# Scaling twelve of sixteen one-hot rows on ScalarE, one u tile ahead on TensorE, four more u tiles in the routing stage

## The reference, cut to what matters

```python
top_s, top_i = lax.top_k(s, PEER_TOPK)                 # s: (token, head, half, 128 keys)
cand_i = top_i[..., 0, :, None] * PEER_NKEYS + top_i[..., 1, None, :]
best_s, pos = lax.top_k(cand_s, PEER_TOPK)             # 16 of 256 sums
eidx = jnp.take_along_axis(cand_i, pos, axis=-1)       # expert = i * 128 + j
gate = jax.nn.softmax(best_s, axis=-1)
a = jax.nn.gelu(jnp.einsum('nd,ned->ne', xt, ue), approximate=False)   # ue = u[eidx]
out = jnp.einsum('ne,ned->nd', a * gt, ve)                             # ve = v[eidx]
```

## Time and profile before

| what | value |
|---|---|
| median of 3 runs | 1917.18 us (1903.87 to 1917.84) |
| the profiled execution | 1917.83 us; its span, first to last instruction, 1916.0 us |
| mean granted clock of PE | 0.959 of full |
| PE busy | 1762.7 us, 92% of the span |
| DVE busy | 1109.7 us, 58% |
| ACT busy | 780.1 us, 41% |
| POOL busy | 954.5 us, 50% |
| gates stage | 745.1 to about 1029 us of the span |
| experts stage | about 1030 to 1916 us |

### The profile page before, as it was taken

The page is one execution under the profiler, slowest core; times in us unless marked ns, Lnnn a source line. Parts: engine busy times, 40 slices in busy tenths (PEclk is TensorE's granted clock), DMA queues, the critical chain, the costliest instruction groups (busy, mean ns, idle before and its releaser), DMA issues. The chain is left out here.

```text
span 1916.0 us, 32083 instructions
## 1 busy us (share of the span) xinstructions
PE 1762.7 (92%) x11464; PEld 1456.3 (76%) x11464; DVE 1109.7 (58%) x2245; ACT 780.1 (41%) x1268; POOL 954.5 (50%) x743
## 2 busy tenths in 40 slices
PE   7979857979999996888998999999999999999996
PEld 5867724449998896888997877778787777878774
DVE  3662678236679999885444545554555545455453
ACT  5333326333333343434443444444444444444442
POOL 3473621006577792000003767666676666766662
PEclk9989969889999997889998999999999999999998
DMA  5211150015444463466777999999999999999995
GB/s 179 99 53 58 18 183 25 1 58 176 158 157 157 124 190 108 160 242 218 228 229 255 328 342 327 335 343 330 329 330 341 338 327 334 326 344 330 333 320 181
DMA packets 166004, 427.22 MB, mean 223 GB/s; under 512 B 23456, under 2 KB 74400, under 8 KB 165280
## 3 DMA queue, kind: packets, MB, share of 16 engines
q1 hardware_dynamic: 118992, 273.20, 43.2%
q0 software_dynamic: 45056, 134.38, 19.0%
q10 hardware_dynamic: 1872, 18.56, 2.4%
HBM read 390.02 MB, written 36.04 MB: 222 GB/s over the span
## 5 line engine op out<-in xcount | busy, mean ns | idle before, releaser
L1740 POOL DMA_INDIRECT rows<-in_peer_v,row_i x256 | 281.8, 1101 | 198.3 <-PE psum L1936 129.9
L1731 POOL DMA_INDIRECT spot<-acts_first,spot_i x256 | 300.5, 1174 | 83.0 <-issue 77.4
L1909 PE MATMUL psum<-h2hi,u_hi 128*128 128x256 f32 x1024 | 294.2, 287 | 8.6 <-DVE u_lo L1802 8.6
L1909 PE MATMUL psum<-h2lo,u_hi 128*128 128x256 f32 x1024 | 291.1, 284 | 0.0
L1909 PE MATMUL psum<-h2hi,u_lo 128*128 128x256 f32 x1024 | 290.4, 284 | 0.0
L1909 PEld LDWEIGHTS psum<-h2hi,u_hi 128*128 128x128 f32 x1024 | 195.9, 191 | 63.0 <-DVE u_lo L1802 31.5
L1919 PE MATMUL psum<-v_hi,w_lo 128*128 128x512 f32 x512 | 202.7, 396 | 0.0
L1919 PE MATMUL psum<-v_lo,w_hi 128*128 128x512 f32 x512 | 202.1, 395 | 0.0
L1919 PE MATMUL psum<-v_hi,w_hi 128*128 128x512 f32 x512 | 201.9, 394 | 0.0
L1802 DVE TENSOR_TENSOR u_lo<-u_raw,u_hi 128x1024 fp32r<-128x1024 f32 x128 | 157.5, 1231 | 71.3 <-ACT u_hi L1755 71.3
L1813 DVE TENSOR_TENSOR wgt<-gel,g_in 128x256 f32<-128x256 f32 x128 | 55.4, 433 | 246.8 <-ACT gel L1765 246.8
(11 more groups left out here) (242 smaller groups left out, 4069.3 us busy)
## 6 DMA issues: line engine op xcount, KB each, us to landing
u_raw<-in_peer_u SPq DMA_DIRECT2D x256, 512.0 KB, 4.2
v_raw<-in_peer_v SPq DMA_DIRECT2D x128, 512.0 KB, 6.6
acts_first<-gel SPq DMA_DIRECT2D x128, 128.0 KB, 2.0
gates<-chunk ACTq DMA_DIRECT2D x4, 4096.0 KB, 12.3
g_in<-gates SPq DMA_DIRECT2D x64, 256.0 KB, 2.9
wring<-in_w_in SPq DMA_DIRECT2D x24, 512.0 KB, 3.6
wq_raw<-in_w_query SPq DMA_DIRECT2D x16, 512.0 KB, 5.7
w_out<-in_w_out SPq DMA_DIRECT2D x1, 4096.0 KB, 18.7
```

The costliest lines, as they stand in the source:

```text
L1731: pool.indirect_dma_start(spot[:, t:t + 1], None, spots, bass.IndirectOffsetOnAxis(ap=spot_i[:, t:t + 1], axis=0)).then_inc(s_spot, 16)
L1740: pool.indirect_dma_start(rows[:, slot, :], None, values, bass.IndirectOffsetOnAxis(ap=row_i[:, t:t + 1], axis=0)).then_inc(s_rows[slot], 16)
L1909: last = pe.matmul(psum[:, ACTS + s % 2, 0:DENSE], a[:, s % 2, k, :], b[:, k, GATHERED:T], start=(k == 0 and a is u_hi and b is h2hi), sto ...
```

## The change

1. In a batch DVE compares twelve tokens of `hot_i` in one operation, without the gate, and ahead of `hot_j`. The other four tokens keep the instruction that compares and multiplies.
2. ACT multiplies those twelve tokens by their gates, in place, one instruction per token, with the gate as a scale on each partition (`scale`). PE waits for this too (`s_scaled`).
3. On ACT the high part of the u tile three ahead comes first in a batch, then `scale`, then Gelu, then the four copies.
4. PE does the u tile of the batch to come ahead of this batch's products; one tile is done ahead of the first batch.
5. `EARLY_ROUTING` goes from 64 to 68: four more u tiles in routing, and four fewer behind the batches (60 in the stage: 16 beside, one more ahead, 43 behind).
6. In the experts stage the four gathers of a quad share a semaphore, and PE waits once for them in place of four times.

```diff
--- before.py
+++ after.py
@@ -53,7 +53,8 @@
 BANKS = 8
 BANK = 512
 
-EARLY_ROUTING = 64
+EARLY_ROUTING = 68
+SCALED = 12
 EARLY = NKEYS
 USLOTS = 4
 QEVERY = 3
@@ -1413,7 +1414,7 @@
         hot_j = sb("hot_j", [P, 2, BATCH, P])
         hot_i = sb("hot_i", [P, 2, BATCH, P])
         chunk = sb("chunk", [P, 2, P, CHUNK])
-        s_gated, s_hot_j = sem("gated_r"), sem("hot_j_r")
+        s_hot_i, s_scaled, s_gated, s_hot_j = sem("hot_i_r"), sem("scaled_r"), sem("gated_r"), sem("hot_j_r")
         s_prod, s_moved = sem("gate_prod"), sem("gate_moved")
         s_st = keep["gates_out"]
         s_u = [sem(f"u4_in{i}") for i in range(USLOTS)]
@@ -1478,10 +1479,11 @@
             def one_hots(eng_it, b):
                 batch = eng_it * BATCHES + b
                 wait(dve, s_prod, (batch - 1) * QUADS)
-                tokens = bass.ds(batch * BATCH + GATHERED, BATCH)
-                dve.tensor_tensor(hot_j[:, b % 2, :, :], iota[:].unsqueeze(1).to_broadcast([P, BATCH, P]),
-                                  chosen[:, 1, tokens].unsqueeze(2).to_broadcast([P, BATCH, P]), ALU.is_equal).then_inc(s_hot_j, 1)
-                for s in range(BATCH):
+                for hot, row, some, ready in ((hot_i, 0, SCALED, s_hot_i), (hot_j, 1, BATCH, s_hot_j)):
+                    dve.tensor_tensor(hot[:, b % 2, 0:some, :], iota[:].unsqueeze(1).to_broadcast([P, some, P]),
+                                      chosen[:, row, bass.ds(batch * BATCH + GATHERED, some)].unsqueeze(2).to_broadcast([P, some, P]),
+                                      ALU.is_equal).then_inc(ready, 1)
+                for s in range(SCALED, BATCH):
                     one = bass.ds(batch * BATCH + GATHERED + s, 1)
                     last = dve.tensor_scalar(hot_i[:, b % 2, s, :], iota[:], chosen[:, 0, one], chosen[:, 2, one],
                                              ALU.is_equal, ALU.mult)
@@ -1517,9 +1519,10 @@
             def body(it):
                 for b in range(BATCHES):
                     batch = it * BATCHES + b
-                    activations(batch, b % USLOTS)
+                    activations(batch + 1, (b + 1) % USLOTS)
+                    pe.wait_ge(s_hot_j, batch + 1)
+                    pe.wait_ge(s_scaled, batch + 1)
                     pe.wait_ge(s_gated, batch + 1)
-                    pe.wait_ge(s_hot_j, batch + 1)
                     for q in range(QUADS):
                         wait(pe, s_moved, (batch - 1) * QUADS + q + 1)
                         for s in range(4):
@@ -1527,10 +1530,13 @@
                                              hot_i[:, b % 2, q * 4 + s, :], start=True, stop=True)
                         last.then_inc(s_prod, 1)
 
+            activations(0, 0)
             body(0)
             with pe.Fori(1, ITERS) as it:
                 body(it)
-            with pe.Fori(BESIDE, TURNS) as it:
+            for e in range(1, USLOTS):
+                activations(BESIDE * USLOTS + e, e)
+            with pe.Fori(BESIDE + 1, TURNS) as it:
                 for e in range(USLOTS):
                     activations(it * USLOTS + e, e)
 
@@ -1552,11 +1558,20 @@
                 wait(act, s_ast[e % 2], (turn * (USLOTS // 2) + e // 2) * 16)
                 act.activation(gel[:, e % 2, 0:GATHERED], psum[:, 6 + e % 2, 0:GATHERED], ACT.Gelu).then_inc(s_gel, 1)
 
+            def scale(it, b):
+                batch = it * BATCHES + b
+                act.wait_ge(s_hot_i, batch + 1)
+                for s in range(SCALED):
+                    one = bass.ds(batch * BATCH + GATHERED + s, 1)
+                    last = act.activation(hot_i[:, b % 2, s, :], hot_i[:, b % 2, s, :], ACT.Identity, scale=chosen[:, 2, one])
+                last.then_inc(s_scaled, 1)
+
             def body(it):
                 for b in range(BATCHES):
                     batch, half = it * BATCHES + b, b // HALF
+                    split_ahead(it * 2 + b // USLOTS, b % USLOTS)
+                    scale(it, b)
                     gelu(it * 2 + b // USLOTS, b % USLOTS)
-                    split_ahead(it * 2 + b // USLOTS, b % USLOTS)
                     if b % HALF == 0:
                         wait(act, s_st[half], it * 16)
                     for q in range(QUADS):
@@ -1634,7 +1649,7 @@
         s_u = [sem(f"u5_in{i}") for i in range(E)]
         s_v = [sem(f"v_in{i}") for i in range(E)]
         s_g = [sem(f"g_in{i}") for i in range(2)]
-        s_rows = [sem(f"rows_in{i}") for i in range(VG)]
+        s_rows = [sem(f"rows_in{z}") for z in range(PER)]
         s_uhi, s_ulo, s_act, s_gel = sem("u5_hi_r"), sem("u5_lo_r"), sem("act5_pe"), sem("gel5_r")
         s_vhi, s_vlo, s_wgt, s_whi, s_wlo = sem("v_hi_r"), sem("v_lo_r"), sem("wgt_r"), sem("w_hi_r"), sem("w_lo_r")
         s_out, s_quad = sem("out_pe"), sem("quad_pe")
@@ -1738,7 +1753,7 @@
                         if q >= PER:
                             pool.wait_ge(s_quad, q - PER + 1)
                         pool.indirect_dma_start(rows[:, slot, :], None, values,
-                                                bass.IndirectOffsetOnAxis(ap=row_i[:, t:t + 1], axis=0)).then_inc(s_rows[slot], 16)
+                                                bass.IndirectOffsetOnAxis(ap=row_i[:, t:t + 1], axis=0)).then_inc(s_rows[q % PER], 16)
 
             pool.wait_ge(s_index, 3)
             gather_spots(0)
@@ -1928,8 +1943,7 @@
                 pe.wait_ge(s_window, q + 1)
                 if kind == "open" and z == 0 and half_of(it, kind):
                     pe.wait_ge(s_acc, 2)
-                for j in range(4):
-                    pe.wait_ge(s_rows[z * 4 + j], it * 16)
+                pe.wait_ge(s_rows[z], it * (16 * 4))
                 for half in range(2):
                     c = slice(half * BANK, (half + 1) * BANK)
                     for j in range(4):
```

## The result

The changed kernel takes 1948.23 us (median of 4 runs, 1937.57 to 1952.01), the kernel before beside it 1910.54 us (1903.87 to 1917.84). The ratio is 1.0178, 95% interval 1.0139 to 1.0217: 1.8% slower. The forecast was 1928 us, no change by over 1%, and the range ended at 1941. The profiled execution took 1952.01 us with a span of 1949.8, so 33.8 us of span are to be found, where the forecast has 10.6.

The account below looks back on a forecast made before the run. The gate batches were to be bound by PE's products alternating with ACT's scalings, the experts stage by PE. 1917.8 + 8.6 (gates stage) + 3 (routing's end) - 1 (edit 6) = 1928 us, range 1899 to 1941.

Parts of the forecast that it names:

- the turn: Gate batches: time from one batch's product start to the next, 10.07 us with the low clock, 8.58 at full clock.
- the price of a scaling: ACT in the gate batches: one scaling every 0.257 us, twelve in 3.21 us, bounds 2.4 and 4.8.
- the stores: Gates stores that ACT issues among the batches: the forecast's turn had no term for them.
- routing's end: End of routing: POOL's work on four more tiles delays DVE's tail by 3 us, bounds 0 and 8.8.
- the tiles behind the batches: End of the gates stage: 43 tiles at 2.89 us each, five fewer than before, 14.5 us less.
- what comes next: Gate batches: PE's products alternate with ACT's scalings, and DVE, at 6.1 us a batch, is no longer late.
- the second rival: Gate batches: low clock lasts through the products, turn 11.6 us, 1953 us; chance 0.18, shared with other slower cases.
- The stage: Gates stage through the last products: 163.6 us against 140.5; with five fewer tiles behind, +8.6 us.
- Edit 6: Experts stage: 1 us less from waiting once per quad, bounds 0 and 5.8 us less.
- dear scalings or a full loss in routing: Part of the slower outcome, with the clock falling: above 1936 us, chance 0.18.
- The clock: Gate batches: PE's clock falls behind gaps of 2.2 us in all batches; the rival that it holds: 1905 us, chance 0.22.

Follow-up runs that it names:

- i_ahead12: Changed kernel with ACT scaling one batch ahead and DVE making the next batch's one-hots ahead of a low part; 1887.33 us, ratio 0.9879.
- k_defer: Changed kernel with two of POOL's low parts moved from routing's end to the gates stage; 1944.49 us, ratio 1.0181.
- m_pe: Kernel before with one edit alone, PE running one u tile ahead of the batch; 1900.52 us, ratio 0.9940.
- b_early64: Changed kernel with 64 u tiles in routing in place of 68; 1940.69 us, ratio 1.0151.
- e_before68: Kernel before with 68 u tiles in routing and nothing else of the change; 1915.31 us, ratio 0.9998.
- l_cast: Kernel before with one edit alone, ACT making the high part first and Gelu second in a batch; 1897.13 us, ratio 0.9925.

## Why the prediction was wrong

The mechanism was right and the sizes were not. No single term puts the result outside the range: the profiled execution lies 11 us above the 1941, and the largest term below is 6.6 us. The steps that failed are four terms of the sum: the turn (the price of a scaling above all), the stores, which I had at nothing, routing's end, and the tiles behind the batches.

**Right: what comes next.** That DVE would stop mattering and PE's products alternate with ACT's scalings is what the trace shows, and what i_ahead12 proves by taking the alternation away. DVE's batch is 6.04 us (754.76 to 760.80; forecast 6.1), PE's gap 2.31 (2.2), the first products come 7.37 us in (7.5), and behind every gap the products are slow (5.44 us or more, where the first batch, behind none, takes 3.74).

**The mean turn was 0.8 us too short, 12 us in all.** Without a store it was 0.56 us. Term by term, forecast and measured: product start to last copy 5.27 and 5.48; copy slot 0.56 and 0.48; cast 0.93 and 0.95; scalings 3.21 and 3.62 from first start to last end; semaphore 0.1 and 0.10. That makes 10.07 and 10.63. The step that failed most is the price of a scaling, 0.41 us a turn and 6.2 us in all. I took it from operations with a PSUM source although I noted that the source is SBUF here: one starts every 3.52 / 12 = 0.293 us, not 0.257. Those operations also write another type, so that the runs don't say which of the two makes the difference. The Trainium skill, "ScalarE: Activation LUTs", section "What ACT_TABLE_LOAD costs", gave 0.29 us, and this case's trace agrees with it; the rule gives the measured pace, and my row did not. The products are 0.21 us a turn, 3.2 in all: I read their slow pace from the batch of 5.23 us in the earlier trace rows, beside which one of 5.47 stands, and the changed kernel's are 5.44.

**The stores were left out.** In front of every fourth cast ACT waits for its own copies and issues the store, three times 0.6 us; PE's gap is then 2.9 to 3.0 us, and in this trace the clock stays low through nearly all of the products behind it (6.65 to 6.70 us, the second rival's mechanism, in 3 of 15). That isn't a rule of the longer gap: in k_defer one of 2.90 us was followed by products of 3.81 us. A store costs 1.8 us here, 0.6 of it on ACT and 1.2 in the clock: the 15 turns took 163.1 us, which is 15 x 10.62, less 1.7 for a first one at full clock, plus 5.5. The stage ran 12.1 us over its forecast.

**Routing gives back more: 6.6 us.** I took +3 with bounds 0 and 8.8; it is 9.64, of which 8.2 is the tail. 1.4 lies ahead of it, and that need not be the change's: the last cast starts anywhere from 712.5 to 718.7 us in the 14 traces. I named four operations in the tail. One had nothing left to lose (line 1325 was slow before), one of the two of line 1231 lost nothing, and two that lose 1.5 and 2.1 us I hadn't listed (lines 1313 and 1332). I also let POOL end at about 743 us, and it ended at 748.2. Line 1313's loss isn't the four tiles' alone: with 64 tiles it took 0.65 us before, but 1.7 to 1.8 in m_pe and b_early64. e_before68, with nothing else changed, loses 7.5 us there. My +3, "the nearest to what a 0.4 us gap of POOL per tile would let through", had no row behind it: the tails of the seven kernels with 68 tiles, from that last cast to the stage's start, take 34.1 to 36.0 us, those of the four with 64 take 27.8 to 29.0, and the three with k_defer's edit 30.7 to 31.0. The Trainium skill, "SBUF — State Buffer", section "SBUF: two separate sides", tells of a port pair that DVE, in some of its operations, and POOL hold for a whole instruction, the other being blocked. This trace agrees: a copy of 0.17 us took 2.32 beside POOL's subtractions, which took 3.15 us each (five in 15.75) where one takes 2.40 alone, while a pair of reductions among them kept its length (2.33).

**Behind the batches: 3.9 us.** I let 43 tiles follow at the old pace, 136.1 us; it was 139.96 (930.44 to 1070.40). The gap is 4.93 us and not 2.70, and the clock falls behind it (0.50 from 944 to 948 us). m_pe shows that PE one tile ahead makes the gap. I had costed that edit at nothing behind the batches.

**Edit 6** comes to 0.4 us (experts, from their first matmul on, 879.4 against 879.8); I took 1. It isn't shown to be worth anything: the same stage takes 879.8 to 882.2 us in the four kernels without it and 878.2 to 885.6 in the ten with it.

The misses add up: 12.1 + 6.6 + 3.9 + 0.6 = 23.2, which is the 33.8 us of span less the forecast's 10.6. All have one sign. (The execution lies 2.2 us above its span, where before it was 1.8; hence 1952.0 and not 1951.2.) For the scalings, routing's end and edit 6 a bound had been written down, and a value near its mild end taken. The forecast's own condition for more, "dear scalings or a full loss in routing", came true in both halves at once, at a chance of 0.18.

**The clock.** That it falls behind gaps of 2.2 us held for this trace, all 15 times. It isn't a rule of the gap's length: in b_early64 a gap of 2.30 us is followed by full pace, one of 2.31 by a slow batch, and five of its fifteen batches behind such gaps are fast; in k_defer four are. So that part of the forecast was in part luck. It may be why the changed kernel's runs spread over 14 us: the fastest, 1937.57 us, had a mean granted clock of 0.957, the other three 0.950 to 0.951. What decides between two equal gaps stays open.

## What to carry to other kernels

Before work is moved to an idle engine, write down that engine's order and follow one item round: if its work for item b stands behind what it does for b - 1, and that waits for another engine which itself waits for the work on b, the two engines take turns, whatever their busy shares say. Move the work one item ahead, and then look for the ring that this closes on the engine that feeds it. Price a new instruction by its own source and form, and where an engine's tail is to run beside POOL, list every operation of the tail, the short ones above all.

## What was new of the hardware

- In one trace (b_early64) PE's gaps of 2.3 us were followed by a product batch of 3.81 us or by one of 5.3 to 5.4. Behind l_cast's gaps of 0.7 to 1.0 us the batch took 3.84 us, 16 times of 16.
- A DVE copy of 128x32 went from 0.17 to 2.32 us beside POOL's subtraction, a `TENSOR_TENSOR` of 128x512 from 0.69 to 2.77; a pair of `TENSOR_REDUCE` took 2.33 both ways.
- One 4 MB store delayed a load of 512 KB so that ACT waited 2.52 us; as four of 1 MB, one a batch, each landing in 4.5 us (median) where the whole took 13.5, the wait was gone from the turns of the batches.
